# Two heads' scores on the two row halves of TensorE, in block one's attention

## The chip, the cores and the metric

The kernel runs on one core of a Trainium2 chip. The metric is the device time of one execution in microseconds (us), and lower is better. A core has TensorE (matrix products, "PE" in the profile, its weight loads "PEld"), VectorE ("DVE"), ScalarE ("ACT"), GpSimd ("POOL") and SyncE ("SP"), which here only issues DMAs. The engines run their own programs in order and wait for each other on semaphores.

## The reference

Three transformer-like blocks over 256 tokens of width 1024. Block one mixes the tokens with attention (8 query heads over 2 key groups, head size 64), a Hyena long convolution and a Fourier mix, merges them under gates, and then runs an expert-choice mixture of 16 experts. Two further layers follow (latent and dilated attention, dense feed-forward). The part that the change touches is block one's attention, with 256 query tokens and 512 keys (256 tokens and 256 context rows):

```python
Q_GROUP = N_Q_HEADS // N_KV_HEADS          # 8 // 2 = 4, so head h uses key group h // 4
def attend(qblk):                          # 128 queries at a time
    s = jnp.einsum('bqkgd,bskd->bkgqs', qblk, k, preferred_element_type=jnp.float32) * scale
    p = jax.nn.softmax(s, axis=-1).astype(v.dtype)
    return jnp.einsum('bkgqs,bskd->bqkgd', p, v)
```

The attention output (512 wide) is later multiplied with the first 512 rows of `w_branch`.

## The kernel before

Each engine has one long program, and the order of work is written out by hand. `P`, `V`, `A`, `G` and `S` are the lanes of TensorE, VectorE, ScalarE, GpSimd and SyncE. `c.x.up()` is a signal, `wait_ge` waits for one, `take(b)` on TensorE waits until bank `b` of PSUM (`PS[:, b, :]`, 512 floats in each of 128 partitions) has been read by whoever `held[b]` names.

**Ahead of attention** TensorE computes the query, key and value projections. `q_half`, `quarter` and `fourier_quarter` are products in three parts (`mm3`, lines 449 to 451), of weights that ScalarE and VectorE split into a high and a low part first (`part()`: ScalarE copies a 1 MB weight tile in two halves of 1024 columns, line 2235, VectorE subtracts, line 1365). Queries are turned by 16 transposes (line 672, four per bank, `j` in 0 to 3, banks 2 and 3 in turn), copied to `QT[0:64]` by ScalarE in four copies. Keys are turned by eight transposes (line 684) into banks 0 and 1 and copied to `kt1` on partitions 0 to 63 by two copies. In `QT` and `kt1` each head, or key group, has partitions 0 to 63 only.

**The attention loop** runs over 16 items `g` (head `h = g // 2`, query block `m = g % 2`), with two trailing steps. On TensorE, item `g` does the score of item `g` (line 698, one fp32 product of 64 rows and 512 columns into bank `g % 2`, after `take(b)`, which waits for the exponential of item `g - 2`), then the four transposes of the probabilities of item `g - 1` (line 707, which wait for the exponential of item `g - 1`), then the value product of item `g - 2` (line 715). VectorE takes the maximum of each score (line 1591), ScalarE the exponential (line 2413), and the two share the copies of the turned probabilities (VectorE line 1599 for even items, ScalarE for odd ones).

**Between these steps** each engine takes one step of a second program, `beside()`, and `step()` does this. TensorE's has 79 steps, of which 48 lie in the loop: the Hyena transposes (`hyena_turn`, line 508), the last quarters of the Hyena projection (`why`), four Fourier quarters, the filter spectrum (line 551), and then for each of 12 gate tiles four quarters, a `mod_products` (line 467) and a `mod_turn` (lines 477, 481). In the loop two items take one gate tile: the even item's steps are `mod_turn`, quarters 1 and 2, the odd item's are quarter 3, `mod_products` and quarter 0 of the next tile. VectorE's and ScalarE's versions hold the matching `part()`, evictions (`gate_out`, line 1416; `mod_evict`, line 1385) and copies, in order with the maxima and exponentials. In the odd item of each pair, VectorE does maximum, `part()`, probability copy, `gate_out`; ScalarE does `part()` of the tile at the end of the even item, and then the odd item's exponential.

**DMAs** are issued by SyncE in one fixed order; each waits until the last user of its buffer is done:

```python
if w.before is not None:
    S.wait_ge(*w.before.used)
S.e.dma_start(w.ap, w.src).then_inc(w.landed[0].sem, 16)
```

In this stage one gate tile and two `wmod` tiles (1 MB each) are loaded per gate. The expert weights (384 tiles of 1 MB) are queued behind them. They go into buffers that become free as block one ends.

Of the kernel before, what the change touches and what calls it, by code (L numbers as in the profile page):

```python
# [81 lines left out]
def program(nc, D, out):  # L82
# [5 lines left out]
    with ExitStack() as ctx:  # L88
# [117 lines left out]
        fx = mix[:, 6:8, :]  # L206
        ev1 = AT
        ev2 = XT2[:, 4:8, :].rearrange("p (i a) b -> p i (a b)", i=2)
        kt1 = XT2[0:64, 0:4, :].rearrange("p (g a) b -> p g (a b)", g=2)
        kn = SS[:, 0, :].rearrange("p (t h d) -> p t h d", t=4, h=2)  # L210
        kv_ps = PS[:, 4:6, :].rearrange("p a (m c) -> p (a m) c", m=2)
        XT1 = gB[:, :, :].rearrange("p a (k c) -> p (a k) c", k=4)
# [218 lines left out]
        def tensor_program():  # L431
# [232 lines left out]
            for q in range(2):  # L664
                quarter("why", 0, 7, q)
            P.wait_ge(c.qn, 2)
            for j in range(4):
                b = 2 + j % 2
                take(b)
                for i in range(2):  # L670
                    for m in range(2):
                        x = t.transpose(PS[0:64, b, i * 256 + m * 128:i * 256 + m * 128 + 128],
                                        QK[:, m, 2 * j + i, 0:64], ident)
                x.then_inc(*c.qtp.up())
                held[b] = [(c.qta, j + 1)]
            for q in range(2, 4):
# [1 line left out]
            for q in range(4):  # L678
                quarter("why", 1, 6, q)
            P.wait_ge(c.kn, 1)  # L680
            for g in range(2):
                take(g)
                for i in range(4):
                    x = t.transpose(PS[0:64, g, i * 128:i * 128 + 128], kn[:, i, g, :], ident)
                x.then_inc(*c.ktp.up())
            held[0], held[1] = [(c.kta, 1)], [(c.kta, 2)]


            P.wait_ge(c.qta, 4)
            for g in range(18):  # L690
                if g < 16:
                    h, m, b = g // 2, g % 2, g % 2
                    take(b)
                    if g == 0:
                        take(4)
                        take(5)
                    P.wait_ge(c.kta, 1 + h // 4)
                    t.matmul(PS[:, b, :], QT[0:64, h, m * 128:m * 128 + 128], kt1[:, h // 4, :],
                             start=True, stop=True).then_inc(*c.sc.up())
                    held[b] = [(c.ex, g + 1)]  # L700
                    step()
                if 0 < g <= 16:
                    b = (g - 1) % 2
                    take(2 + b)
                    P.wait_ge(c.ex, g)
                    for i in range(4):
                        x = t.transpose(PS[:, 2 + b, i * 128:i * 128 + 128], PB[:, b, i * 128:i * 128 + 128], ident)
                    x.then_inc(*c.ptp.up())
                    held[2 + b] = [(c.pca, (g - 1) // 2 + 1) if b else (c.pcv, (g - 1) // 2 + 1)]
                    step()  # L710
                if g > 1:
                    h, m, b = (g - 2) // 2, g % 2, g % 2
                    take(2 + b)
                    for i in range(4):
                        x = t.matmul(PS[:, 4 + m, h * 64:h * 64 + 64], PT[:, b, i * 128:i * 128 + 128],
                                     VV[:, i, (h // 4) * 64:(h // 4) * 64 + 64], start=i == 0, stop=i == 3)
                    x.then_inc(*c.pv.up())
                    step()
            held[4], held[5] = [(c.at, 1)], [(c.at, 2)]
# [352 lines left out]
            for l in range(2):  # L1072
# [32 lines left out]
                def latent_heads():  # L1105

                    for src, b0, j0 in ((KK, 2, 0), (QK2, 4, 0), (KK, 2, 2), (QK2, 4, 2)):
                        for j in (j0, j0 + 1):
                            b = b0 + j % 2
                            take(b)  # L1110
                            if src is KK:
                                P.wait_ge(c.kk, 2 * l + 2)
                                P.wait_ge(c.kua, 2 * l + 2)
                            else:
                                P.wait_ge(c.qr, l + 1)
                            for i in range(2):
                                for m in range(2):
                                    x = t.transpose(PS[0:96, b, i * 256 + m * 128:i * 256 + m * 128 + 128],
                                                    src[:, m, 2 * j + i, :], ident[:, :])
                            x.then_inc(*c.qtp.up())  # L1120
                            n = (c.qtp.n - 5) // 2
                            held[b] = [(c.qta, n + 5) if j % 2 else (c.qtv, n + 1)]

                def q_up(m, b):
                    w = W["wqu", l]
# [10 lines left out]
                def kv_up(m, b):  # L1136
                    w = W["wkvu", l]
                    P.wait_ge(*w.landed)
                    P.wait_ge(c.kta, l + 3)
                    for i in range(2):  # L1140
                        take(b + i)
                        t.matmul(PS[:, b + i, :], KT[:, 2, m * 128:m * 128 + 128], w.ap[:, i * 512:i * 512 + 512],
                                 start=True, stop=True).then_inc(*c.ku.up())
                        held[b + i] = [(c.kua if i else c.kuv, 2 * l + m + 1)]
# [14 lines left out]
                for m in range(2):  # L1159
                    P.wait_ge(c.kr, 2 * l + m + 1)  # L1160
                    for k in range(3):
                        x = t.transpose(PS[:, 2 + k // 2, (k % 2) * 256 + m * 128:(k % 2) * 256 + m * 128 + 128],
                                        lat[:, m, k * 128:k * 128 + 128], ident[:, :])
                        if m and k:
                            x.then_inc(*c.ktp.up())
                held[2], held[3] = [(c.ktv, l + 1)], [(c.kta, l + 3)]
                dilated(1, 0, 6)
                held[6] = [(c.ds, 4 * l + 3)]
                q_up(0, 2)
# [10 lines left out]
                def scores(g):  # L1180
# [2 lines left out]
                    take(b)  # L1183
                    if g == 0:
                        P.wait_ge(c.qtv, 4 * l + 4)
                        P.wait_ge(c.qta, 4 * l + 8)
                    if g == 6:
                        P.wait_ge(c.dqv, 2 * l + 2)
                        P.wait_ge(c.dqa, 2 * l + 2)
# [127 lines left out]
        def vector_program():  # L1317
# [267 lines left out]
            for g in range(18):  # L1585
# [15 lines left out]
                if g > 1:  # L1601
                    m = g - 16
                    if m >= 0:
                        V.wait_ge(c.ex, 15 + m)
                        own(v.reciprocal(den[:, 0, m, :], den[:, 0, m, :]))
                        V.wait_ge(c.pv, 15 + m)
                        own(v.tensor_tensor(AT[:, m, :].rearrange("p (h d) -> p h d", h=8),
                                            PS[:, 4 + m, :].rearrange("p (h d) -> p h d", h=8),
                                            den[:, 0, m, :].unsqueeze(2).to_broadcast([128, 8, 64]),
                                            ALU.mult).then_inc(*c.at.up()), c.at)  # L1610
                    step()
# [399 lines left out]
            for l in range(2):  # L2011
# [52 lines left out]

                def latent_heads():
                    for i, (dst, b, j) in enumerate(((KT, 2, 0), (QT2, 4, 0), (KT, 2, 2), (QT2, 4, 2))):
                        V.wait_ge(c.qtp, 8 * l + 5 + 2 * i)
                        own(v.tensor_copy(dst[0:96, 2 * j:2 * j + 2, :].rearrange("p a b -> p (a b)"),
                                          PS[0:96, b, :]).then_inc(*c.qtv.up()), c.qtv)

# [3 lines left out]
                latent(1)  # L2074
                split_to(tile("wid", 6 * l) + 4)
                dilated(0, 0, 0)
                V.wait_ge(c.ktp, 2 * l + 3)
                for k in range(2):
                    i = v.tensor_scalar(KT[:, k, :], PS[:, 2, k * 256:k * 256 + 256], gT[:, 80 + 3 * l + k:81 + 3 * l + k],
                                        None, ALU.mult)  # L2080
# [142 lines left out]
        def scalar_program():  # L2223
# [10 lines left out]
            def copy(o, i):  # L2234
                return a.activation(o, i, ACT.Copy)  # L2235
# [156 lines left out]
                             ACT.Square).then_inc(*c.hsq.up()), c.hsq)  # L2392
            own(copy(VV[:, :, :], kv_ps[:, :, 128:256]).then_inc(*c.vvd.up()), c.vvd)
            own(a.activation(T1[:, 1023:1024], mhalf[:, 0:1], ACT.Exp))
            for j in range(4):
                A.wait_ge(c.qtp, j + 1)
                own(copy(QT[0:64, 2 * j:2 * j + 2, :].rearrange("p a b -> p (a b)"),
                         PS[0:64, 2 + j % 2, :]).then_inc(*c.qta.up()), c.qta)
            hyena_in(0, 7)
            part()  # L2400
            for g in range(2):
                A.wait_ge(c.ktp, g + 1)
                own(copy(kt1[:, g, :], PS[0:64, g, :]).then_inc(*c.kta.up()), c.kta)


            step()
            for g in range(18):
                if g < 16:
                    h, m, b = g // 2, g % 2, g % 2
                    A.wait_ge(c.nmx, g + 1)  # L2410
                    if g > 1:
                        A.wait_ge(c.ptp, g - 1)
# [166 lines left out]
            for l in range(2):  # L2579
# [23 lines left out]

                def latent_heads():
                    for i, (dst, b, j) in enumerate(((KT, 3, 1), (QT2, 5, 1), (KT, 3, 3), (QT2, 5, 3))):
                        A.wait_ge(c.qtp, 8 * l + 6 + 2 * i)
                        own(copy(dst[0:96, 2 * j:2 * j + 2, :].rearrange("p a b -> p (a b)"),
                                 PS[0:96, b, :]).then_inc(*c.qta.up()), c.qta)

# [18 lines left out]
                A.wait_ge(c.ktp, 2 * l + 4)  # L2628
# [283 lines left out]
def layout(I):  # L2912
# [17 lines left out]
    d["wq"] = blocks(w[:, 0:512], 4, 512)  # L2930
# [3 lines left out]
    d["wbr"] = blocks(I["w_branch"][0], 8, 256)  # L2934
# [61 lines left out]
```

## Time and profile before

| | |
|---|---|
| runs | 2323.64 us median of 3 (2322.56 to 2324.06) |
| the profiled execution | span 2322.8 us; it is one execution, and 0.8 us below the median of the runs |
| PE, PEld | 2004.6 us (86%), 1339.8 us (58%) |
| DVE, ACT, POOL | 983.5 us (42%), 669.8 us (29%), 66.9 us (3%) |
| data moved | 647.48 MB, mean 279 GB/s |

PE busy is the time in which at least one matmul record is open; a record's end is modelled, so a stretch of dense records shows as busy. The start of one record to the start of the next is the better measure of what an instruction costs. An fp32 product has two records (`x2` for one product), a transpose or a product of split (fp32r) data has one. The page's second part cuts the span into 40 slices of 58 us, and attention lies in the second to fourth.

### The profile page before, as it was taken

What the parts mean: (1) busy time and instruction counts of PE and PEld (TensorE: products, weight loads), DVE (VectorE), ACT (ScalarE), POOL (GpSimd) and SP (SyncE); (2) the same over time, 40 slices, a digit from 0 to 9 for tenths busy, and PEclk for the clock granted to TensorE, in tenths of its full rate; (3) what the DMA queues carried; (4) which work ended last, traced back from release to release, by engine and by line L of the source; (5) the groups of instructions that cost most, each with busy time, mean ns of one, the idle gap of its engine ahead of it and who ended that gap; (6) DMA issues with size and microseconds to landing.
All of it is one profiled execution on the core that took longest, in us unless ns stands there. A gap on an engine that the chain in (4) does not pass through costs nothing.

```text
span 2322.8 us, 29242 instructions
## 1 busy us (share of the span) xinstructions
PE 2004.6 (86%) x12336; PEld 1339.8 (58%) x12336; DVE 983.5 (42%) x1219; ACT 669.8 (29%) x812; POOL 66.9 (3%) x144
## 2 busy tenths in 40 slices
PE   6999999666666666666678999999999999999998
PEld 4767972111111111111136999779998999788997
DVE  3744661000000000000004656876658666876656
ACT  3433430000000000000003444564435444465444
POOL 0000000000000000000001000000001000100000
PEclk8999999777777777777799999999999999999999
DMA  7345899999999999999998565335554554415552
GB/s 305 120 175 203 336 377 420 421 420 421 420 421 421 421 421 420 421 421 421 421 421 333 186 206 173 132 118 182 193 190 161 182 194 168 171 78 186 193 190 89
DMA packets 91363, 647.48 MB, mean 279 GB/s; under 512 B 10144, under 2 KB 10656, under 8 KB 14304
## 3 DMA queue, kind: packets, MB, share of 16 engines
q1 hardware_dynamic: 91232, 645.61, 71.1%
q8 instruction: 97, 1.59, 0.3%
q14 instruction: 34, 0.28, 0.0%
HBM read 644.52 MB, written 1.05 MB: 278 GB/s over the span
## 4 chain that ended last, share of the span: by engine, by line
PE 53%; DMA 19%; SPq 17%; DVE 6%; ACT 2%; issue 2%; POOL 0%; DVEq 0%; ACTq 0%; POOLq 0%
SPq L2823 16%; PE PS L449 14%; PE PS L451 13%; PE PS L450 13%; DMA XR<-in_mu 4%; DMA front<-in_mu 3%; PE PS L907 3%; DMA QT<-in_mu 2%; DMA ring<-in_mu 2%; DMA XT<-in_mu 2%; DMA ring<-in_fg 2%; DMA XT<-in_md 1%; DMA c_dft<-in_mu 1%; DVE low L1846 1%; PE PS L885 1%
## 5 line engine op out<-in xcount | busy, mean ns | idle before, releaser
L1846 DVE TENSOR_TENSOR low<-ring,WH 128x2048 fp32r<-128x2048 f32 (+1 forms) x163 | 372.1, 2283 | 181.6 <-ACT WH L2235 179.0
L449 PE MATMUL PS<-XH,WH 128*128 128x256 f32 x1408 | 397.4, 282 | 3.6 <-DVE XL L1878 3.5
L450 PE MATMUL PS<-XL,WH 128*128 128x256 f32 x1408 | 395.8, 281 | 0.0
L451 PE MATMUL PS<-XH,low 128*128 128x256 f32 x1408 | 393.5, 279 | 0.0
L2235 ACT ACTIVATE WH<-ring 128x2048 fp32r<-128x2048 f32 (+1 forms) x164 | 313.1, 1909 | 28.9 <-DMA ring<-in_fg 22.8
L449 PEld LDWEIGHTS PS<-XH,WH 128*128 128x128 f32 x1408 | 265.0, 188 | 7.2 <-issue 5.4
L451 PEld LDWEIGHTS PS<-XH,low 128*128 128x128 f32 x1408 | 268.0, 190 | 0.0
L450 PEld LDWEIGHTS PS<-XL,WH 128*128 128x128 f32 x1408 | 265.1, 188 | 1.4
L1828 DVE TENSOR_TENSOR T1S<-T1S,PS 128x512 f32<-128x512 f32 x16 | 11.0, 688 | 534.2 <-PE PS L907 534.2
L2503 ACT ACTIVATE T1S<-PS 128x512 f32<-128x512 f32 x16 | 9.6, 597 | 546.9 <-PE PS L907 546.8
L1836 DVE TENSOR_TENSOR T1S<-PS,ATG 128x512 f32<-128x512 f32 x32 | 22.1, 692 | 278.8 <-PE PS L942 278.1
L449 PE MATMUL PS<-WH,FH 128*128 128x512 f32 x352 | 139.7, 397 | 0.4 <-DVE FL L1976 0.4
L451 PE MATMUL PS<-WH,FL 128*128 128x512 f32 x352 | 138.6, 394 | 0.0
L450 PE MATMUL PS<-low,FH 128*128 128x512 f32 x352 | 138.5, 393 | 0.0
L907 PE MATMUL PS<-ring,big 128*32 128x512 f32 x600 | 98.6, 762 | 39.7 <-DMA ring<-in_mu 22.6
L449 PE MATMUL PS<-WH,XH 128*128 128x512 f32 (+1 forms) x256 | 104.7, 409 | 4.4 <-DVE low L1846 3.4
L942 PE MATMUL PS<-ring,PBT 128*32 128x512 f32 x312 | 70.2, 773 | 39.5 <-DMA XT<-in_md 19.4
L450 PE MATMUL PS<-low,XH 128*128 128x512 f32 (+1 forms) x256 | 99.6, 389 | 0.0
L451 PE MATMUL PS<-WH,XL 128*128 128x512 f32 (+1 forms) x256 | 99.5, 389 | 0.0
L2235 ACT ACTIVATE PBT<-PS 128x256 f32<-128x256 f32 (+1 forms) x25 | 11.5, 461 | 298.6 <-PE PS L927 290.3
L907 PEld LDWEIGHTS PS<-ring,big 128*32 128x32 f32 x600 | 15.5, 119 | 116.5 <-DMA ring<-in_mu 63.0
L2568 ACT ACTIVATE T1S<-GA 128x512 f32<-128x512 f32 x44 | 27.8, 632 | 184.9 <-DVE GA L1964 184.9
(453 smaller groups left out, 3127.1 us busy)
## 6 DMA issues: line engine op xcount, KB each, us to landing
ring<-in_fg SPq DMA_DIRECT2D x44, 1024.0 KB, 4.9
ring<-in_fu SPq DMA_DIRECT2D x44, 1024.0 KB, 5.0
ring<-in_fd SPq DMA_DIRECT2D x44, 1024.0 KB, 4.9
ring<-in_mu SPq DMA_DIRECT2D x39, 1024.0 KB, 26.7
ring<-in_md SPq DMA_DIRECT2D x39, 1024.0 KB, 27.1
ring<-in_mg SPq DMA_DIRECT2D x36, 1024.0 KB, 27.2
ring<-in_wmod SPq DMA_DIRECT2D x24, 1024.0 KB, 6.2
ahead<-in_mg SPq DMA_DIRECT2D x14, 1024.0 KB, 27.4
```

Of the source, the lines that this page charges most:

```text
L449: t.matmul(o, l[0], r[0], start=start, stop=False, skip_group_check=True)
L450: t.matmul(o, l[0], r[1], start=False, stop=False, skip_group_check=True)
L451: return t.matmul(o, l[1], r[0], start=False, stop=stop, skip_group_check=True)
L885: x = t.matmul(PS[:, bank, at:at + 32 * (e1 - e0)], XN[:, m, k * 128:k * 128 + 128], big[:, m * 512 + 32 * e0:m * 512 + 32 * e1], start=m ...
L907: x = t.matmul(PS[32 * j:32 * j + 32, b, :], (XG0[:, k, ex * 32:ex * 32 + 32] if ex < 2 else XG2[:, k, ex * 32 - 64:ex * 32 - 32]), w.ap[: ...
L942: x = t.matmul(PS[32 * j:32 * j + 32, n, :], PT[:, 0, i * 128 + 32 * j:i * 128 + 32 * j + 32], ws[j // 2].ap[:, j % 2, n * 512:n * 512 + 5 ...
L1828: own(v.tensor_tensor(HH, SG, PS[:, 1, :], ALU.mult).then_inc(*c.hh.up()), c.hh)
L1836: own(v.tensor_tensor(T1[:, h], PS[:, n, :], gB[:, 1, h], ALU.mult).then_inc(*c.yv.up()), c.yv)
L1846: own(v.tensor_tensor(low[:, w.slot.index, 0:size], w.flat, WH[:, w.slot.index, 0:size].bitcast(f32), ALU.subtract).then_inc(*c.wl.up()), ...
L2235: return a.activation(o, i, ACT.Copy)
L2568: own(a.activation(SS[:, n % 2, :], GA[:, n % 2, :], ACT.Silu).then_inc(*c.si.up()), c.si)
L2823: S.e.dma_start(w.ap, w.src).then_inc(w.landed[0].sem, 16)
```

## The change

Heads are taken in pairs, of which one has key group 0 and the other key group 1. The host orders the columns of `wq` and the rows of `w_branch` so that the pair (reference heads `p` and `p + 4`) lies side by side. A pair of heads is turned by one transpose of 128 columns (8 transposes in place of 16, two copies of 128 partitions in place of four of 64), both key groups by one (4 in place of 8, one copy in place of two, of all 128 partitions). The even head and key group 0 are then on partitions 0 to 63, the odd head and key group 1 on 64 to 127. In the loop, item `g` is now query block `g // 2 % 2` of head `2 * (g // 4) + g % 2`. Scores are issued at even items only, two at a time, into banks 0 and 1, after both banks have been read. The rest is the same: one maximum, one exponential, four transposes, one copy and one value product for each item, with the same steps of `beside()` at the same places.

```diff
-            for j in range(4):
-                b = 2 + j % 2
+            for j in range(2):
+                b = 2 + j
                 take(b)
                 for i in range(2):
                     for m in range(2):
-                        x = t.transpose(PS[0:64, b, i * 256 + m * 128:i * 256 + m * 128 + 128],
-                                        QK[:, m, 2 * j + i, 0:64], ident)
+                        h = 4 * j + 2 * i
+                        x = t.transpose(PS[:, b, i * 256 + m * 128:i * 256 + m * 128 + 128],
+                                        QK[:, m, h:h + 2, :].rearrange("p h d -> p (h d)"), ident)
...
-            for g in range(2):
-                take(g)
-                for i in range(4):
-                    x = t.transpose(PS[0:64, g, i * 128:i * 128 + 128], kn[:, i, g, :], ident)
-                x.then_inc(*c.ktp.up())
-            held[0], held[1] = [(c.kta, 1)], [(c.kta, 2)]
+            take(0)
+            take(1)
+            for i in range(4):
+                x = t.transpose(PS[:, 0, i * 128:i * 128 + 128], kn[:, i, :, :].rearrange("p h d -> p (h d)"), ident)
+            x.then_inc(*c.ktp.up())
+            held[0] = [(c.kta, 1)]
...
                 if g < 16:
-                    h, m, b = g // 2, g % 2, g % 2
-                    take(b)
                     if g == 0:
                         take(4)
                         take(5)
-                    P.wait_ge(c.kta, 1 + h // 4)
-                    t.matmul(PS[:, b, :], QT[0:64, h, m * 128:m * 128 + 128], kt1[:, h // 4, :],
-                             start=True, stop=True).then_inc(*c.sc.up())
-                    held[b] = [(c.ex, g + 1)]
+                        P.wait_ge(c.kta, 1)
+                    if g % 2 == 0:
+                        pair, m = g // 4, g // 2 % 2
+                        take(0)
+                        take(1)
+                        for i in range(2):
+                            s = slice(64 * i, 64 * i + 64)
+                            t.matmul(PS[:, i, :], QT[s, pair, m * 128:m * 128 + 128], kt1[s, :],
+                                     start=True, stop=True).then_inc(*c.sc.up())
+                            held[i] = [(c.ex, g + i + 1)]
                     step()
...
                 if g > 1:
-                    h, m, b = (g - 2) // 2, g % 2, g % 2
+                    m, b = (g - 2) // 2 % 2, g % 2
+                    h = 2 * ((g - 2) // 4) + b
                     take(2 + b)
                     for i in range(4):
                         x = t.matmul(PS[:, 4 + m, h * 64:h * 64 + 64], PT[:, b, i * 128:i * 128 + 128],
-                                     VV[:, i, (h // 4) * 64:(h // 4) * 64 + 64], start=i == 0, stop=i == 3)
+                                     VV[:, i, b * 64:b * 64 + 64], start=i == 0, stop=i == 3)
...
-                        V.wait_ge(c.ex, 15 + m)
+                        V.wait_ge(c.ex, 14 + 2 * m)
                         own(v.reciprocal(den[:, 0, m, :], den[:, 0, m, :]))
-                        V.wait_ge(c.pv, 15 + m)
+                        V.wait_ge(c.pv, 14 + 2 * m)
...
-            for j in range(4):
+            for j in range(2):
                 A.wait_ge(c.qtp, j + 1)
-                own(copy(QT[0:64, 2 * j:2 * j + 2, :].rearrange("p a b -> p (a b)"),
-                         PS[0:64, 2 + j % 2, :]).then_inc(*c.qta.up()), c.qta)
+                own(copy(QT[:, 2 * j:2 * j + 2, :].rearrange("p a b -> p (a b)"),
+                         PS[:, 2 + j, :]).then_inc(*c.qta.up()), c.qta)
             hyena_in(0, 7)
             part()
-            for g in range(2):
-                A.wait_ge(c.ktp, g + 1)
-                own(copy(kt1[:, g, :], PS[0:64, g, :]).then_inc(*c.kta.up()), c.kta)
+            A.wait_ge(c.ktp, 1)
+            own(copy(kt1, PS[:, 0, :]).then_inc(*c.kta.up()), c.kta)
...
+    turned = lambda a: a.reshape(-1, 2, 4, 64).transpose(0, 2, 1, 3).reshape(-1, 512)
+    d["wq"] = blocks(turned(w[:, 0:512]), 4, 512)
...
+    d["wbr"] = blocks(np.concatenate([turned(wb[0:512].T).T, wb[512:]], axis=0), 8, 256)
```

The remaining edits renumber the later waits on `qta`, `qtp`, `kta` and `ktp`, whose counts are smaller by two, two, one and one.

## Rows read from the trace of the kernel before

**Rows 1.** Stretches of the span: us; PE, PEld, DVE, ACT, POOL busy; clock; DMA share; GB/s.
```profile
28.00:35.00 7.00, 6.09 (x14) 4.89 (x15) 3.37 (x9) 1.32 (x3) 0.00 (x0) 0.52 1.02 424
152.00:166.00 14.00, 14.00 (x98) 10.09 (x97) 5.46 (x7) 5.71 (x10) 0.00 (x0) 1.00 0.59 225
190.00:270.00 80.00, 78.75 (x566) 66.52 (x565) 48.89 (x69) 28.42 (x33) 0.00 (x0) 1.00 0.64 244
330.00:1190.00 860.00, 591.43 (x3168) 131.36 (x3166) 58.15 (x107) 19.77 (x39) 9.59 (x33) 0.78 1.01 420
```

**Rows 2.** SyncE's waits, 60 to 330 us: total us, times, longest.
```profile
SPq L2823 <- PE PS L451: 199.8, 23, 24.5
```

**Rows 3.** Timeline of TensorE, one gate's steps in the loop: start, us.
```profile
141.86 0.39 PE L449 MATMUL PS<-XTH,low 128*128 128x256 f32 x1 [0.58 <-DVE big L1416]
143.49 1.12 PE L698 MATMUL PS<-XT,QT 64*128 64x512 f32 x2
144.54 1.13 PE L481 MATMUL PS<-XT,middles 128*128 128x512 f32 x2
145.51 0.60 PE L707 MATMUL PS<-base,PBT 128*128 128x128 f32 x4
...
152.37 0.60 PE L707 MATMUL PS<-base,PBT 128*128 128x128 f32 x4
152.90 1.92 PE L467 MATMUL PS<-ring,c2s 128*32 128x512 f32 x16
154.75 1.11 PE L715 MATMUL PS<-filters,PBT 128*128 128x64 f32 x8
155.66 0.37 PE L449 MATMUL PS<-XTH,low 128*128 128x256 f32 x1
```

**Rows 4.** Timeline of TensorE, the records open in 138.30 to 138.50 us.
```profile
138.32 0.64 PE L467 MATMUL PS<-ring,c2s 128*32 128x512 f32 x4
```

**Rows 5.** Timeline of TensorE from the query transposes to the first scores.
```profile
83.06 1.03 PE L672 MATMUL PS<-base,ATG 128*64 128x128 f32 x8
84.39 1.25 PE L672 MATMUL PS<-base,ATG 128*64 128x128 f32 x8 [0.30 <-ACT QT L2235]
85.40 0.37 PE L449 MATMUL PS<-XTH,low 128*128 128x256 f32 x1
...
93.98 1.03 PE L684 MATMUL PS<-base,T1S 128*64 128x128 f32 x8
95.37 1.09 PE L698 MATMUL PS<-XT,QT 64*128 64x512 f32 x2 [0.35 <-issue]
96.39 0.65 PE L508 MATMUL PS<-base,XN 128*128 128x128 f32 x4
```

**Rows 6.** Timeline of ScalarE: Hyena copy and first exponential, and a later gate.
```profile
97.14 0.60 ACT L2235 ACTIVATE mix<-PS 128x512 f32<-128x512 f32 x1 [1.25 <-PE PS L508]
98.12 0.69 ACT L2413 ACTIVATE PBT<-PS,nm 128x512 f32<-128x512 f32 x1 [0.38 <-DVE nm L1591]
...
177.84 2.15 ACT L2235 ACTIVATE low<-ring 128x1024 fp32r<-128x1024 f32 x2 [3.35 <-DMA ring<-in_wgt]
180.02 0.69 ACT L2413 ACTIVATE PBT<-PS,nm 128x512 f32<-128x512 f32 x1
```

**Rows 7.** Timeline of VectorE: around the first maximum, and in the loop's last gate.
```profile
94.82 2.48 DVE L1365 TENSOR_TENSOR low<-ring,low 128x1024 fp32r<-128x1024 f32 x2
97.33 0.69 DVE L1591 TENSOR_REDUCE nm<-PS 128x1 f32<-128x512 f32 x1
...
193.06 2.49 DVE L1365 TENSOR_TENSOR low<-ring,low 128x1024 fp32r<-128x1024 f32 x2
196.31 0.69 DVE L1416 COPY big<-PS 128x512 f32<-128x512 f32 x1
```

**Rows 8.** Timeline of TensorE: 16 records of line 601, after an idle time and without one.
```profile
28.91 6.72 PE L601 MATMUL PS<-ring,ATG 128*128 128x256 f32 x16 [1.58 <-DVE ATG L1329]
71.50 3.72 PE L601 MATMUL PS<-ring,XT 128*128 128x256 f32 x16
```

More of the change, by code:

```diff
@@ L208, in program @@
         ev2 = XT2[:, 4:8, :].rearrange("p (i a) b -> p i (a b)", i=2)
-        kt1 = XT2[0:64, 0:4, :].rearrange("p (g a) b -> p g (a b)", g=2)
+        kt1 = XT2[:, 0:2, :].rearrange("p a b -> p (a b)")
         kn = SS[:, 0, :].rearrange("p (t h d) -> p t h d", t=4, h=2)
@@ L680, in tensor_program @@
             P.wait_ge(c.kn, 1)
-            for g in range(2):
-                take(g)
-                for i in range(4):
-                    x = t.transpose(PS[0:64, g, i * 128:i * 128 + 128], kn[:, i, g, :], ident)
-                x.then_inc(*c.ktp.up())
-            held[0], held[1] = [(c.kta, 1)], [(c.kta, 2)]
-            P.wait_ge(c.qta, 4)
+            take(0)
[4 more added lines that the diff above has]
+            held[0] = [(c.kta, 1)]
+            P.wait_ge(c.qta, 2)
             for g in range(18):
                 if g < 16:
-                    h, m, b = g // 2, g % 2, g % 2
-                    take(b)
                     if g == 0:
@@ L1120, in latent_heads @@
                             x.then_inc(*c.qtp.up())
-                            n = (c.qtp.n - 5) // 2
-                            held[b] = [(c.qta, n + 5) if j % 2 else (c.qtv, n + 1)]
+                            n = (c.qtp.n - 3) // 2
+                            held[b] = [(c.qta, n + 3) if j % 2 else (c.qtv, n + 1)]
                 def q_up(m, b):
@@ L1138, in kv_up @@
                     P.wait_ge(*w.landed)
-                    P.wait_ge(c.kta, l + 3)
+                    P.wait_ge(c.kta, l + 2)
                     for i in range(2):
@@ L1165, in tensor_program @@
                             x.then_inc(*c.ktp.up())
-                held[2], held[3] = [(c.ktv, l + 1)], [(c.kta, l + 3)]
+                held[2], held[3] = [(c.ktv, l + 1)], [(c.kta, l + 2)]
                 dilated(1, 0, 6)
@@ L1185, in scores @@
                         P.wait_ge(c.qtv, 4 * l + 4)
-                        P.wait_ge(c.qta, 4 * l + 8)
+                        P.wait_ge(c.qta, 4 * l + 6)
                     if g == 6:
@@ L2066, in latent_heads @@
                     for i, (dst, b, j) in enumerate(((KT, 2, 0), (QT2, 4, 0), (KT, 2, 2), (QT2, 4, 2))):
-                        V.wait_ge(c.qtp, 8 * l + 5 + 2 * i)
+                        V.wait_ge(c.qtp, 8 * l + 3 + 2 * i)
                         own(v.tensor_copy(dst[0:96, 2 * j:2 * j + 2, :].rearrange("p a b -> p (a b)"),
@@ L2076, in vector_program @@
                 dilated(0, 0, 0)
-                V.wait_ge(c.ktp, 2 * l + 3)
+                V.wait_ge(c.ktp, 2 * l + 2)
                 for k in range(2):
@@ L2408, in scalar_program @@
                 if g < 16:
-                    h, m, b = g // 2, g % 2, g % 2
+                    m, b = g // 2 % 2, g % 2
+                    h = 2 * (g // 4) + b
                     A.wait_ge(c.nmx, g + 1)
@@ L2605, in latent_heads @@
                     for i, (dst, b, j) in enumerate(((KT, 3, 1), (QT2, 5, 1), (KT, 3, 3), (QT2, 5, 3))):
-                        A.wait_ge(c.qtp, 8 * l + 6 + 2 * i)
+                        A.wait_ge(c.qtp, 8 * l + 4 + 2 * i)
                         own(copy(dst[0:96, 2 * j:2 * j + 2, :].rearrange("p a b -> p (a b)"),
@@ L2627, in scalar_program @@
                 split_to(tile("wid", 6 * l) + 4)
-                A.wait_ge(c.ktp, 2 * l + 4)
+                A.wait_ge(c.ktp, 2 * l + 3)
                 own(a.activation(KT[:, 2, :], PS[:, 3, 0:256], ACT.Copy, scale=gT[:, 82 + 3 * l:83 + 3 * l]).then_inc(*c.kta.up()),
@@ L2933, in layout @@
     d["wgt"] = blocks(w[:, 1792:4864], 8, 256)
-    d["wbr"] = blocks(I["w_branch"][0], 8, 256)
+    wb = I["w_branch"][0]
+    d["wbr"] = blocks(np.concatenate([turned(wb[0:512].T).T, wb[512:]], axis=0), 8, 256)
     d["wout"] = blocks(I["w_out"][0], 4, 512)
```

1 line of the change is left out of this document (removed).

## The prediction

> **What bounds the kernel now.** I looked first at stretches of the span [rows 1]. In the attention stage TensorE is busy all the time (14.00 of 14.00 us, clock 1.00) while the DMA engines are busy 0.59 of it and VectorE and ScalarE under half. From 190 to 270 us it is the same (78.75 of 80, DMA 0.64). From 330 to 1190 us, the experts, DMA is at 1.01 and 420 GB/s, and TensorE is not the limit. So attention is bound by TensorE, and what comes behind it by DMA. Does time saved in the first reach the end? The waits of SyncE say so [rows 2]: up to 330 us it spends 199.8 us waiting for products of line 451. The loads are released by TensorE, there is DMA time to spare up to 270 us, and the experts' bytes are a fixed amount, so if the releases come X earlier, the saturated stage begins and ends X earlier, and the layers behind it too. I take the whole of what is saved by 200 us as saved at the end.
>
> The price of each step is read from the timeline of one gate [rows 3]: from the start of one group to the start of the next. A score costs 144.54 - 143.49 = 1.05 us. One gate (two items) takes 155.66 - 141.86 = 13.80 us.
>
> **The change, part by part.**
>
> *Two scores at once.* This is the disputed price: no row shows two products on the two row halves. The nearest rows are the `mod_products`, eight fp32 products of 512 columns on column quarters of the array. They take 154.75 - 152.90 = 1.85 us together, 0.23 us each, against 1.05 for the score alone. Inside one [rows 4], four records start at once and, in the first 0.18 us, nothing else: these are the first records of four different products, so the second record of a product doesn't hold up the first of the next one. Bounds: at best the second score is free (eight times 1.05 = 8.4 us saved), at worst it costs what a product costs when it follows another, 145.51 - 144.54 = 0.97 us (8 times 0.08 = 0.6 us saved). By its nearness to rows 4 I take the best, less 0.1 us for eight second starts: 8.3 us.
>
> The Trainium skill ("TensorE: Matmul & The Clock Gate", Part 3: Packing small matmuls) says that products on different row groups run concurrently, but also that matmuls start and end strictly in program order. By the strict rule the second record of the first score would hold back the first record of the second; rows 4 speak against it on column tiles, and no row shows row tiles. What it would give is the second rival below.
>
> *Turning queries and keys.* Query transposes: 16 took 85.40 - 83.06 = 2.34 us, with 0.30 waiting for a bank [rows 5]. Eight of full width and no wait for a bank: about 1.0 us (a group of eight shows 1.03). That is 1.3 us less. VectorE's split of the next `why` tile has its own pace and will hold TensorE for about 0.15 us of it: 1.15 us earlier at the keys. Keys: from the first transpose to the first score 95.37 - 93.98 = 1.39 us, most of it the wait for a copy after the first four transposes, and that remains: the second four lay in its shadow. No gain, no loss. ScalarE saves three copies of 0.6 us in a stretch where it waits for TensorE (1.25 us ahead of the Hyena copy [rows 6]): nothing.
>
> *Covers that go.* The odd score stood between other steps and hid waits. With it gone:
> - After the first pair the Hyena turn's bank must be copied by ScalarE before the next quarter may write it. The copy ends 97.74 - 96.39 = 1.35 us after the turn began [rows 5, 6], and the turn itself takes 0.6: a wait of 0.8 us, which the score of item 1 covered.
> - The maximum of item 0 is tied to VectorE's split, which ends at 97.30, not to TensorE [rows 7]; the exponential ends at 98.81 plus its readout, 98.9 [rows 6]. TensorE comes to its transposes at about 98.2 and waits another 0.75 us.
> - The second Hyena turn, ahead of item 3: the same copy, 0.9 us. The Fourier copy ahead of the filter spectrum: 0.1 us.
>
> Sum of these: 2.6 us. Queued behind each are only TensorE's own later steps.
>
> *The new wait.* An even item now waits for the exponential of the item just before, where it waited for the one before that. In the steady part that exponential comes behind ScalarE's split of a gate tile, which waits for a DMA. In [rows 6] the split starts at 177.84 when the tile lands, the exponential of item 13 ends at about 180.9, and the score of item 14 starts at 143.49 + 3 x 13.80 = 184.9 [rows 3]. With the period shorter by 1.05 us that is 183.85: 2.9 us to spare, so no wait. In items 2 to 7 no split waits for a DMA, and the maxima no longer wait for a late score.
>
> *The gate evictions.* At 141.86 TensorE waited 0.58 us for VectorE's eviction, behind its maximum, split and copy [rows 3]. The maximum of item 7 no longer waits for a score, so this chain starts about 1 us sooner and the wait goes: 0.6 us gained. In the last gate the split starts at 193.06 and the eviction ends at 197.00 [rows 7], just when TensorE needs it (141.86 + 4 x 13.80 = 197.06). TensorE will want it 1.05 us sooner, and the chain can't follow all the way: the tile lands at about 177.84 + 13.8 = 191.6, ScalarE's second half ends 2.15 later at 193.8, then 1.24 + 0.7 + 0.7 for VectorE gives 196.45 against 196.0. I take 0.4 us lost. The host's new order of `wq` and `w_branch` costs nothing on the chip, and value products and transposes keep their number and shapes.
>
> **Sum:** 8.3 + 1.15 - 2.6 + 0.6 - 0.4 = 7.05 us. The profiled span 2322.8 becomes 2315.75; it stands 0.8 us below the median of the runs, so the runs give 2316.6.
>
> **The rivals.**
>
> 1. *The two halves don't overlap.* The second score costs 0.97. Then 8 x 0.97 = 7.8 less 0.1 is lost again, the wait for the first exponential (0.75) and the late eviction (0.4) are covered again: 7.05 - 7.7 + 1.15 = +0.5 us, 2323.1. For it: no row shows row halves side by side. Against: rows 4. Here the change doesn't do what it says.
>
> 2. *They overlap by half.* If records start strictly in order, the second record of the first score and the first record of the second run together and the other two alone: three record times in place of two, about 0.5 us for the second score. 8 x 0.5 = 4.0 lost, about 0.9 covered again: 3.9 us faster, 2319.7. Against it: the four starts at once in rows 4.
>
> 3. *The clock falls.* The waits of 0.9 us ahead of the first pair, 0.8 and 0.75 lie within 6 us. At 27 to 35 us, after an idle of 1.58 us (and shorter ones before), the granted clock of the stretch was 0.52, the 1.2 GHz level, and 16 records took 6.72 us against 3.72 at full clock [rows 1, 8]: 3.0 us. So 7.05 - 3.0 = 4.05, 2319.6, or some 1.5 us less if it is short, 2318.1. For it: three waits close together; against: none is as long as 1.58.
>
> 4. *Slower than before: the DMA behind ScalarE.* TensorE's pair waits for an exponential that stands behind a wait for a gate tile, in four gates. There are 2.9 us to spare; each us beyond that in a landing costs 1 us per gate. To eat 7.05 us, tiles must land 2.9 + 7.05 / 4 = 4.7 us later than now. Were it 6 us, four gates lose 3.1 each: 7.05 - 12.4, 5.3 us slower, 2329.0. For it: ScalarE waits 3.35 us for such a tile [rows 6]. Against: the same 3 MB per gate in 12.75 in place of 13.80 us raise the DMA share from 0.59 only to 0.64 [rows 1], and releases move with TensorE.
>
> **How the numbers follow.** Full overlap at full clock 0.62; clock falls 0.12; half overlap 0.10; none 0.12; slower 0.04 (4 and everything like it). The likeliest gives 2316.6, and its own range is 2314.5 to 2318.5, from covers mis-sized by 2 us. The range reaches over half overlap and the clock to 2322.0 and leaves out rivals 1 and 4 (0.16) and little below 2314.5. About 0.2% (4.65 us) is what a measurement of this kernel can tell from no change. Faster than 2319.0 are nearly all of the likeliest (0.6), two thirds of the clock case (0.08) and little of half overlap (0.02): 0.70. Slower 0.04, the same 0.26.
>
> **What would show it.** Line 698 in pairs: four records within 1.1 us before the next group starts (right), 1.5 (rival 2) or 2.0 (rival 1). Line 672 with eight records. Waits of TensorE after line 508 for ScalarE's copies, and one for the exponential of item 0. A gate period of 12.75 us. The `mod_products` of item 15 at about 187 us, not at 152.90 + 3 x 13.80 = 194.3; the first records of line 907 earlier by the same. The prediction is wrong if pairs take over 1.3 us, if the clock in 93 to 105 us is below 1.00, or if the gain at 200 us isn't there at 330 and at 1190 us, since then a transfer that doesn't follow TensorE sets the experts' start.

## The result, and the profile after

The changed kernel takes 2316.55 us (median of 6 runs, 2315.46 to 2321.8), the kernel before 2323.85 (median of 6, 2322.56 to 2325.22). The ratio is 0.9969, with a 95% interval of 0.9959 to 0.9979, so 7.3 us faster. 2316.6 was forecast. The profiled execution is not a typical one: its span is 2318.2 us (2319.47 with what lies around it). What it lost is shown below; a second profile (e6) has 2314.7.

TensorE around the first scores, timeline of the changed kernel, start and us:

```profile
82.95 1.03 PE L673 MATMUL PS<-base,ATG 128*128 128x128 f32 x8
83.74 0.36 PE L449 MATMUL PS<-XTH,low 128*128 128x256 f32 x1
...
92.74 0.60 PE L685 MATMUL PS<-base,T1S 128*128 128x128 f32 x4
94.17 1.13 PE L703 MATMUL PS<-XT,QT 64*128 64x512 f32 x4 [0.84 <-ACT XT L2241]
95.23 0.66 PE L508 MATMUL PS<-base,XN 128*128 128x128 f32 x4
...
98.84 0.66 PE L712 MATMUL PS<-base,PBT 128*128 128x128 f32 x4 [0.52 <-ACT PBT L2419]
...
107.48 0.38 PE L449 MATMUL PS<-low,XTH 128*128 128x256 f32 x1 [0.75 <-ACT mix L2241]
```

Queries are turned in 83.74 - 82.95 = 0.79 us, where it was 2.34 [rows 5]. A pair of scores (four records) takes 95.23 - 94.17 = 1.06 us, what one score took. The other rows are the covers that went: TensorE waits for the key copy, for the first exponential, and for the copy behind the second Hyena transposes. From the first key transpose to the first score it is 94.17 - 92.74 = 1.43 us, 1.39 before [rows 5]: the second four key transposes had indeed lain in the shadow of the copy.

One gate of the loop, same view, to be read beside [rows 3]:

```profile
137.94 0.38 PE L449 MATMUL PS<-XTH,low 128*128 128x256 f32 x1
...
139.56 1.13 PE L703 MATMUL PS<-XT,QT 64*128 64x512 f32 x4
140.62 1.13 PE L481 MATMUL PS<-XT,middles 128*128 128x512 f32 x2
...
144.25 0.37 PE L449 MATMUL PS<-XTH,low 128*128 128x256 f32 x1
...
147.17 0.60 PE L712 MATMUL PS<-base,PBT 128*128 128x128 f32 x4
147.70 1.92 PE L467 MATMUL PS<-ring,c2s 128*32 128x512 f32 x16
149.55 1.10 PE L721 MATMUL PS<-filters,PBT 128*128 128x64 f32 x8
150.47 0.37 PE L449 MATMUL PS<-XTH,low 128*128 128x256 f32 x1
...
163.67 0.39 PE L449 MATMUL PS<-XTH,low 128*128 128x256 f32 x1 [0.51 <-DVE big L1422]
...
190.07 0.38 PE L449 MATMUL PS<-XTH,low 128*128 128x256 f32 x1 [1.18 <-DVE big L1422]
```

The wait of 0.58 us that stood ahead of the first of these rows [rows 3] is no longer recorded. The gate takes 150.47 - 137.94 = 12.53 us in place of 13.80. VectorE evicts the gate tiles with even numbers, and two of its three evictions in the loop are waited for (0.51 and 1.18). The two records that are open right at the start of a pair, from a window of 139.5 to 140.0 us:

```profile
139.56 0.70 PE L703 MATMUL PS<-XT,QT 64*128 64x512 f32 x2
```

Two first records open together, and the second ones only behind them, as in [rows 4].

Where the stage ends, and where the profiled execution lost something (the spectrum products behind the loop; a gate quarter behind them; stretches with their busy times, clock, DMA share and GB/s):

```profile
197.56 3.62 PE L736 MATMUL PS<-mix,c_dft 128*128 128x256 f32 x16
...
241.27 0.39 PE L449 MATMUL PS<-XTH,low 128*128 128x256 f32 x1 [2.27 <-ACT big L2241]
```

```profile
152.00:166.00 14.00, 13.49 (x100) 9.87 (x98) 6.60 (x8) 4.28 (x7) 0.00 (x0) 1.00 0.70 254
190.00:270.00 80.00, 77.22 (x546) 66.89 (x547) 45.81 (x67) 28.70 (x33) 0.00 (x0) 0.98 0.64 239
330.00:1190.00 860.00, 585.85 (x3160) 127.40 (x3160) 54.99 (x99) 18.97 (x38) 9.60 (x33) 0.78 1.01 420
238.00:246.00 8.00, 5.73 (x33) 3.79 (x26) 3.14 (x3) 5.42 (x6) 0.00 (x0) 0.79 0.98 349
242.00:245.40 3.40, 3.40 (x13) 2.37 (x12) 0.17 (x2) 2.11 (x2) 0.00 (x0) 0.52 0.94 378
```

The spectrum products start at 197.56 us; in the kernel before the row is

```profile
204.54 3.62 PE L730 MATMUL PS<-mix,c_dft 128*128 128x256 f32 x16
```

6.98 us later. At 241.27 us TensorE then waited 2.27 us for ScalarE, which stood behind the landing of a gate tile, and the granted clock of 238 to 246 us was 0.79. From 242.0 to 245.4 us it was 0.52, the 1.2 GHz level, right behind that idle time. The stretch of the experts is as before, 420 GB/s [rows 1].

### The profile page after: what moved, and what is told of

Same layout as the page of the kernel before. It is cut to its first block, busy times and chain, and to the rows that moved or that the text cites. A ratio compares the mean times of both kernels' runs of the same rounds, so it can differ in the third digit from the quotient of the medians.

```text
span 2318.2 us, 29211 instructions
## 1 busy us (share of the span) xinstructions
PE 1992.0 (86%) x12324; PEld 1333.8 (58%) x12324; DVE 983.3 (42%) x1219; ACT 668.0 (29%) x809; POOL 66.8 (3%) x144
## 3 DMA queue, kind: packets, MB, share of 16 engines
HBM read 644.52 MB, written 1.05 MB: 278 GB/s over the span
## 4 chain that ended last, share of the span: by engine, by line
PE 52%; DMA 19%; SPq 17%; DVE 7%; ACT 3%; issue 2%; POOL 1%; DVEq 0%; ACTq 0%; POOLq 0%
SPq L2829 16%; PE PS L449 14%; PE PS L451 13%; PE PS L450 13%; DMA front<-in_mu 4%; DMA XR<-in_mu 3%; PE PS L913 3%; DMA QT<-in_mu 2%; DMA ring<-in_mu 2%; DMA XT<-in_mu 2%; DMA ring<-in_wgt 1%; DMA XT<-in_md 1%; DMA c_dft<-in_mu 1%; DMA ring<-in_fg 1%; DVE low L1852 1%
## 5 line engine op out<-in xcount | busy, mean ns | idle before, releaser
L948 PE MATMUL PS<-ring,PBT 128*32 128x512 f32 x312 | 75.0, 829 | 31.9 <-DMA ring<-in_md 16.1
```

The costliest lines, as they stand in the source:

```text
L948: x = t.matmul(PS[32 * j:32 * j + 32, n, :], PT[:, 0, i * 128 + 32 * j:i * 128 + 32 * j + 32], ws[j // 2].ap[:, j % 2, n * 512:n * 512 + 5 ...
```

## The experiments

A common measure for all: from the first query transpose to the first spectrum product, in the profile of each. It leaves out by how much the loads ahead of attention vary. Before 204.54 - 83.06 = 121.48 us; changed kernel 197.56 - 82.95 = 114.61.

**e1: two scores together, on one row half.** The kernel before, with only the order of its scores changed.

```diff
-                    h, m, b = g // 2, g % 2, g % 2
-                    take(b)
+                    h = g // 2
...
-                    P.wait_ge(c.kta, 1 + h // 4)
-                    t.matmul(PS[:, b, :], QT[0:64, h, m * 128:m * 128 + 128], kt1[:, h // 4, :],
-                             start=True, stop=True).then_inc(*c.sc.up())
-                    held[b] = [(c.ex, g + 1)]
+                    if g % 2 == 0:
+                        take(0)
+                        take(1)
+                        P.wait_ge(c.kta, 1 + h // 4)
+                        for i in range(2):
+                            t.matmul(PS[:, i, :], QT[0:64, h, i * 128:i * 128 + 128], kt1[:, h // 4, :],
+                                     start=True, stop=True).then_inc(*c.sc.up())
+                            held[i] = [(c.ex, g + i + 1)]
```

> The kernel before, with its layout, transposes and copies, but the scores of two items issued together at even items, both from partitions 0 to 63 (the two query blocks of one head). Theory (the gain is the overlap on the two row halves): the second score costs about 0.97 us behind the first, the four records of a pair start about 0.5 us apart, a pair takes 2.0 us, and the time is that of the kernel before within 2 us (0.6 gained by back-to-back issue, 0.6 by the first gate eviction, about 1.5 lost in covers). Rival (the gain comes from issuing two scores at once, so that maxima and exponentials are earlier): 4 us or more faster than before.

Measured: 2323.37 us (11 runs, 2322.29 to 2324.8) against 2323.91 (21 runs); ratio 0.9997 (0.9988 to 1.0006): no difference. Stage 203.57 - 82.77 = 120.80 us. The timeline of TensorE for a pair, whole and in a window that ends at 116.7 us, and the cover that went:

```profile
99.03 0.38 PE L449 MATMUL PS<-XTH,low 128*128 128x256 f32 x1 [0.75 <-ACT mix L2238]
...
115.80 1.12 PE L701 MATMUL PS<-XT,QT 64*128 64x512 f32 x2
...
115.80 1.98 PE L701 MATMUL PS<-XT,QT 64*128 64x512 f32 x4
...
203.57 3.62 PE L733 MATMUL PS<-mix,c_dft 128*128 128x256 f32 x16
```

On one half the four records run one behind the other (one begun in the first 0.5 us, two in the first 0.9, all four over 1.98 us), on two halves in 1.13 us. Nothing else differs for the pair, so the rival of e1 falls: two scores issued together on one half leave the median where it was and the stage 0.68 us shorter (121.48 - 120.80), of the 6.87 of the change. The overlap carries the gain.

**e2: turned in pairs, scores alone.** The changed kernel, with each score at its own item.

```diff
-                    if g % 2 == 0:
-                        pair, m = g // 4, g // 2 % 2
-                        take(0)
-                        take(1)
-                        for i in range(2):
-                            s = slice(64 * i, 64 * i + 64)
-                            t.matmul(PS[:, i, :], QT[s, pair, m * 128:m * 128 + 128], kt1[s, :],
-                                     start=True, stop=True).then_inc(*c.sc.up())
-                            held[i] = [(c.ex, g + i + 1)]
+                    pair, m, i = g // 4, g // 2 % 2, g % 2
+                    take(i)
+                    s = slice(64 * i, 64 * i + 64)
+                    t.matmul(PS[:, i, :], QT[s, pair, m * 128:m * 128 + 128], kt1[s, :],
+                             start=True, stop=True).then_inc(*c.sc.up())
+                    held[i] = [(c.ex, g + 1)]
```

> The changed kernel with its turned queries and keys and its two halves of partitions, but each score issued alone at its own item, as before. Theory: only the query transposes' 1.2 us are gained, the covers stay and so does the first gate's wait of 0.6 us: 1.2 us faster than before, scores at 1.05 us each on either half. Rival (turning two heads at once carries the gain): 5 us or more faster.

Measured: 2322.58 us (11 runs, 2321.83 to 2326.49), ratio 0.9997 (0.9988 to 1.0006). Stage 203.22 - 82.40 = 120.82 us, 0.66 shorter, about half of what was expected. The rival (turning carries the gain) falls. The medians differ by 1.3 us, and the interval reaches from 2.8 us faster to 1.4 slower.

```profile
93.63 1.09 PE L700 MATMUL PS<-XT,QT 64*128 64x512 f32 x2 [0.84 <-ACT XT L2238]
...
98.30 0.66 PE L709 MATMUL PS<-base,PBT 128*128 128x128 f32 x4 [0.32 <-ACT PBT L2416]
...
203.22 3.62 PE L733 MATMUL PS<-mix,c_dft 128*128 128x256 f32 x16
```

The second row shows where the rest went. Counted from the first query transpose, TensorE is 1.08 us earlier at the first score and 0.60 at the first transposes of probabilities, because it waits 0.32 us for the first exponential, whose maximum goes by VectorE's pace [rows 7].

**e3: the eviction ahead of the split.** The changed kernel, and in VectorE's `beside()`:

```diff
+                        if n in (0, 2, 4) and q == 3:
+                            gate_out(n, 7)
                         if n < 11 and q == (3 if n < 8 else 1):
                             part()
...
                     if n < 8:
-                        gate_out(n, 7)
+                        if n not in (0, 2, 4):
+                            gate_out(n, 7)
                         yield 1
```

> The changed kernel, with VectorE's eviction of gates 0, 2 and 4 ahead of its split of the next tile, not behind it and the probability copy. Theory (TensorE's waits of 0.51 and 1.18 us ahead of quarter 0 of gates 3 and 5 are the eviction standing behind the split, which waits for its tile's DMA): both waits go, 1.7 us faster than the changed kernel in the profile at 200 us. Rival (TensorE's next want is the split itself, or the DMA): the wait moves to line 449 behind VectorE's line 1371 and the time stays.

Measured: 2314.71 us (5 runs, 2313.18 to 2315.55), ratio 0.9960 (0.9947 to 0.9972). Stage 194.58 - 82.43 = 112.15 us, 2.46 shorter than in the changed kernel's first profile and 2.09 than in its second. No wait of line 449 for VectorE's eviction is left between 82 and 207 us, and none for line 1371 in its place but the one of 0.2 us ahead of the loop. VectorE in that gate:

```profile
159.10 0.69 DVE L1422 COPY big<-PS 128x512 f32<-128x512 f32 x1 [4.19 <-PE PS L451]
159.82 2.49 DVE L1371 TENSOR_TENSOR low<-ring,low 128x1024 fp32r<-128x1024 f32 x2
162.35 0.69 DVE L1608 COPY PBT<-PS 128x512 f32<-128x512 f32 x1
...
194.58 3.62 PE L736 MATMUL PS<-mix,c_dft 128*128 128x256 f32 x16
```

The rival falls. More is gained than the two recorded waits, 1.69 us, because a third gate was late without a recorded wait: quarter 0 of gate 1 starts 137.94 - 136.76 = 1.18 us behind the value product in the changed kernel and 137.12 - 136.21 = 0.91 here. And behind the two waits the whole loss, from start to start, is larger than the idle time, as the table further on has it.

**e4: other work in the uncovered places.** The changed kernel, with TensorE's steps in the first items at other places:

```diff
                     if g == 0:
                         take(4)
                         take(5)
+                        step()
                         P.wait_ge(c.kta, 1)
...
-                    step()
+                    if g not in (0, 3):
+                        step(2 if g == 1 else 1)
                 if 0 < g <= 16:
...
-                    step()
+                    if g not in (1, 3):
+                        step()
                 if g > 1:
...
                     x.then_inc(*c.pv.up())
-                    step()
+                    step(3 if g == 3 else 1)
```

> The changed kernel, with other work put into the places where TensorE waits since the odd scores are gone: the first Hyena transposes ahead of the first pair of scores, two quarters ahead of the first transposes of probabilities, and transposes and value product of items 2 and 1 between the second Hyena transposes and the first Fourier quarter. Theory (the covers cost 0.75 + 0.52 + 0.75 us in the changed kernel): TensorE's waits for ScalarE's copies and the first exponential go, 1.5 to 2 us less at 121 us. Rival (VectorE's chain of splits and maxima sets the pace there): waits come back further on, ahead of the Fourier quarters or the filter spectrum, and less than 0.5 us is gained.

Measured: 2314.69 us (5 runs, 2314.56 to 2316.87), ratio 0.9961 (0.9947 to 0.9974). Stage 196.90 - 83.57 = 113.33 us: 1.28 and 0.91 shorter than in the two profiles of the changed kernel, between the theory's 1.5 and the rival's 0.5. At 121 us, where the theory put its 1.5 to 2 us, it is 1.15 less: the transposes of probabilities there start 120.51 - 83.57 = 36.94 us behind the first query transpose, 121.04 - 82.95 = 38.09 in the changed kernel. The three waits are gone, two others are there:

```profile
95.45 0.63 PE L508 MATMUL PS<-base,XN 128*128 128x128 f32 x4 [1.48 <-DVE XN L1416]
96.01 1.13 PE L704 MATMUL PS<-XT,QT 64*128 64x512 f32 x4
...
117.29 1.96 PE L551 MATMUL PS<-big,c_dft 128*128 128x512 f32 x4 [0.97 <-ACT mix L2244]
...
189.39 0.39 PE L449 MATMUL PS<-XTH,low 128*128 128x256 f32 x1 [1.64 <-DVE big L1425]
...
196.90 3.40 PE L739 MATMUL PS<-mix,c_dft 128*128 128x256 f32 x15
```

The first is where the wait for the key copy was (0.84), and longer; the second is new, a copy of ScalarE that stands behind its probability copy. The last eviction, 1.18 and 0.94 us in the two profiles of the changed kernel, is waited for 1.64 here. So VectorE's and ScalarE's chains do take a part back.

**e5: both edits, and ScalarE's Fourier copy one step earlier.**

```diff
-                for _ in range(4):
+                for _ in range(3):
                     yield 1
                 A.wait_ge(c.fn, 1)
                 own(copy(fx, PS[:, 6, :].rearrange("p (a b) -> p a b", a=2)).then_inc(*c.fx.up()), c.fx)
+                yield 1
                 hyena_out(2, 7)
```

> The two edits before this one together (early evictions, other work in the uncovered places), and ScalarE's Fourier copy one step earlier, ahead of the probability copy, for the wait of 0.97 us ahead of the filter spectrum that moving the covers left. Theory (each wait is TensorE's own and they add): 1.7 + 1.2 + 0.9 = 3.8 us less than the changed kernel at 200 us, and 2312.8 us. Rival (the loop is by then bound by the landing of the gate tiles, so that what is gained early is waited for later): the waits reappear as line 449 behind line 1371, and the time is no lower than 2314.5 us.

Measured: 2312.43 us (5 runs, 2311.61 to 2313.08) against 2324.28 (10 runs); ratio 0.9951 (0.9937 to 0.9965), 2312.8 was expected. Stage 192.63 - 81.88 = 110.75 us, 3.86 shorter than in the first profile of the changed kernel (3.8 expected) and 3.49 than in the second. The gains of e3 (2.1 to 2.5) and e4 (0.9 to 1.3) add. That the sum also met 3.8 is partly luck: e3 gave more than its 1.7, and the wait ahead of the filter spectrum fell from 0.97 only to 0.36 us where all of it was expected to go. The rival falls: no wait for the split is recorded in the loop. It is the fastest version here.

**e6: the changed kernel again.**

> The changed kernel once more, without an edit, for a second profiled execution and for the spread. Theory (the profiled execution of the changed kernel lost 2.4 us against its median behind attention, where a gate tile landed 1.5 us late and the clock fell for a moment, and both vary from execution to execution): median 2316 to 2317, start of the spectrum products at about 197.5 us again, and a wait for ScalarE's eviction at about 240 us of 0.8 to 1.6 us with the clock at 1.00. Rival (the change itself brings the late landing): a wait of over 2 us there again, and a median of 2318 or more.

Measured: 2315.85 us (6 runs, 2315.38 to 2322.95), ratio 0.9971 (0.9959 to 0.9982). Stage 196.68 - 82.44 = 114.24 us. Timeline and stretches:

```profile
196.68 3.62 PE L736 MATMUL PS<-mix,c_dft 128*128 128x256 f32 x16
...
239.30 0.39 PE L449 MATMUL PS<-XTH,low 128*128 128x256 f32 x1 [1.19 <-ACT big L2241]
```

```profile
190.00:270.00 80.00, 78.37 (x572) 68.59 (x571) 48.41 (x69) 32.10 (x39) 0.00 (x0) 1.00 0.67 257
```

The median is a little below the 2316 to 2317 expected, the spectrum products start 0.8 us before the expected 197.5, and the rival falls. The same wait is 1.19 us here, with the clock at 1.00. It is 1.29 in e1 and 1.58 in e2, which are as slow as the kernel before, and 0.81 in the profile of the kernel before itself. So the 2.27 us with a fallen clock is not in every execution of the changed kernel: from 197.56 to the first residual product of the experts (326.58 us) the first profile takes 129.02 us, the second 323.34 - 196.68 = 126.66. The 2.36 us between them are nearly the difference of its time to the median, 2319.47 - 2316.55 = 2.9. One of its runs (2321.8) and one of e6's (2322.95) were still longer and have no profile. So three of the twelve runs of the changed kernel lie 2.9 us or more above their median, and one of the 37 of the kernel before; whether the change makes such executions more frequent, and why, is open.

## Why the prediction was right, point by point

**What bounds, and whether a gain reaches the end.** Right. SyncE still waits 196.0 us for line 451 up to 330 us (199.8 before [rows 2]), the experts run at the same 420 GB/s, and in e6 the gain is over 7 us at every mark: spectrum products 204.54 - 196.68 = 7.86 (0.6 of which lies ahead of attention), experts 330.85 - 323.34 = 7.51, span 2322.8 - 2314.7 = 8.1. One part of it was too simple: that the loads move with TensorE. ScalarE's split of the last gate's tile, which starts when the tile has landed, starts 191.44 - 184.92 = 6.52 us earlier, and TensorE is 8.31 earlier by then (7.40 and 8.94 in e6).

**Two scores at once.** Right, and shown: 1.06 us for a pair on two halves against 1.91 on one (e1, 117.71 - 115.80). The best of the two bounds held, and rows 4, a row of column quarters, foretold row halves. Rivals 1 (no overlap) and 2 (half) fall. The Trainium skill ("TensorE: Matmul & The Clock Gate", Part 3: Packing small matmuls) says that products on different row groups run concurrently, and that matmuls start strictly in program order. With the first of these the trace agrees (1.06 us for the pair). If a product's second record counted as the next one in that order, a pair would have taken 1.5 us; the trace has two records start together at 139.56 us, and no third before 140.0.

**Turning.** The size was off in two ways. Eight transposes took 0.79 us and not 1.0, which was read from the 1.03 of [rows 5], the length of the group with the modelled end of its last record; the row of the changed kernel has the same 1.03. And TensorE waited 0.20 us for VectorE's split, 0.15 forecast: the first score comes 95.37 - 94.17 = 1.20 us earlier (1.15 forecast; 0.11 of it were there before the transposes). Alone, though, turning is worth only 0.66 us (e2).

**Covers that go.** Right in place and nearly in size: 0.75, 0.52 and 0.75 us where 0.8, 0.75 and 0.9 were forecast. The 0.1 ahead of the filter spectrum did not come: it starts 1.14 us behind the value product in both kernels.

**The sum, from start to start.** The forecast and what came of it, between the same instructions of the two kernels (step `g` is the loop's; "transposes" are those of the probabilities):

| stretch | before | changed | gained | forecast |
|---|---|---|---|---|
| first query transpose to first score | 12.31 | 11.22 | 1.09 | 1.15 |
| first score to transposes of step 3, with two odd scores and the covers | 14.56 | 14.82 | -0.26 | -0.4 |
| the six further odd scores, steps 5 to 15 | 44.42 | 36.86 | 7.56 | 6.1 |
| transposes of step 7 to score of step 8 (first gate eviction) | 5.70 | 5.18 | 0.52 | 0.6 |
| transposes of step 11 to score of step 12 | 4.97 | 5.63 | -0.66 | 0 |
| transposes of step 15 to those of step 16 (last gate eviction) | 4.86 | 6.19 | -1.33 | -0.4 |

These add to 6.92 us, and what lies between them gives -0.05: 6.87. The third row adds up six intervals: from the filter spectrum products ahead of the odd score (steps 5 and 7), or from the even score (steps 9 to 15), to the transposes of the odd step. In e6 the rows give 1.08, -0.26, 7.55, 0.51, -0.54 and -1.09.

**The odd score was under-priced.** This is one of the two terms that were mis-sized most. TensorE in the kernel before:

```profile
148.18 0.37 PE L449 MATMUL PS<-XTH,low 128*128 128x256 f32 x1
...
149.57 0.28 PE L451 MATMUL PS<-XTH,low 128*128 128x256 f32 x1
149.77 1.12 PE L698 MATMUL PS<-XT,QT 64*128 64x512 f32 x2
150.82 0.39 PE L449 MATMUL PS<-XTH,low 128*128 128x256 f32 x1
151.05 0.28 PE L450 MATMUL PS<-XTL,low 128*128 128x256 f32 x1
151.17 0.29 PE L451 MATMUL PS<-XTH,low 128*128 128x256 f32 x1
```

From quarter 2 to the transposes of the odd item it was 152.37 - 148.18 = 4.19 us; it is 147.17 - 144.25 = 2.92, 1.27 less and not 1.05. Split products follow each other by 0.12 us. The score starts 0.20 us behind the last of them, and the first two behind the score start 0.23 apart: together the 0.2 us. All six odd scores from step 5 on gave 1.25 to 1.27 us, about 1.5 more in sum than forecast.

**The gate evictions.** The first wait (0.58) went, and gave 0.52, though e3 shows that 0.27 was still to be had there. The last one was forecast at 0.4 us and measured 1.18 (0.94 in e6), and there was one more, of 0.51 (0.40), where none was forecast. The cause forecast, VectorE's eviction behind a split that waits for its tile, was right (e3). VectorE in the last gate of the changed kernel:

```profile
186.08 2.48 DVE L1371 TENSOR_TENSOR low<-ring,low 128x1024 fp32r<-128x1024 f32 x2 [5.17 <-ACT low L2241]
188.59 0.69 DVE L1605 COPY PBT<-PS 128x512 f32<-128x512 f32 x1
189.32 0.69 DVE L1422 COPY big<-PS 128x512 f32<-128x512 f32 x1
```

Two sizes were off: TensorE comes 1.27 us sooner in each gate and not 1.05, and the tiles' landings follow it by less (6.52 us earlier for 8.31); the DMA share of 152 to 166 us rose to 0.70 where 0.64 was worked out. From start to start these two gates lose 1.99 us where 0.4 was forecast. This and the term before cancel: 1.5 us more gained, 1.6 more lost. That the median fell within 0.1 us of 2316.6 is therefore partly luck; the range didn't need it.

**The new wait on the previous exponential.** No row of line 703 waits for an exponential; the only wait there is for the key copy. Rival 4 (slower, an exponential behind ScalarE's wait for a landing) did not come. The landings reached TensorE by VectorE's evictions instead, with recorded waits of 1.7 us in all.

**The clock.** Rival 3 didn't come at 93 to 105 us (1.00 in all eight profiles). It came once, at 242 us, after a wait of 2.27 us.

The sum forecast for the stage was 7.05 us; measured between the same marks it is 121.48 - 114.61 = 6.87, and 7.24 in e6.

## What to carry to other kernels

Two fp32 products of 64 rows cost the time of one here, on the two row halves, into two banks and issued back to back (other ways to place them were not tried, but for one row half); the layout that makes it possible cost nothing, since the host orders the weights (e2). Before taking an instruction out, list what it hid: here 2.0 of some 10 us came back as three waits that the odd scores had covered, and putting other work there returned half of it. When the bounding engine gets faster, look for evictions that stand behind a wait for a DMA on another engine: moving three of them ahead of the split was worth 2.1 to 2.5 us. And prices are read from start to start: the length of a group with a modelled end (1.03 for 0.79), and idle times alone (1.69 for 1.99), both missed.

## What was not expected of the hardware

- A score between two runs of split products costs 1.27 us and not its own 1.05: it starts 0.08 us late behind the run ahead of it, and the run behind it starts slower by 0.11.
- Two scores on one half, issued back to back, take 1.91 us and not twice 1.05, nor the 1.05 + 0.97 of the forecast's worst case.
- Transposes of 128 columns are no slower than of 64: eight take 0.79 us, and each group of eight has a length of 1.03 us on the timeline, of 64 columns [rows 5] or of 128. The eight of 64 that took 85.40 - 84.39 = 1.01 us from start to start stood behind an idle time.
